# A closer spacing of the expert-row dots of half A beside half B's first mixer and queries: 226 of them ahead of half B's picks, where there were 138

## The reference, cut to what matters

```python
top_s, top_i = lax.top_k(s, PEER_TOPK)
...
best_s, best_pos = lax.top_k(cand_s.reshape(T, PEER_HEADS, PEER_TOPK * PEER_TOPK), PEER_TOPK)
...
u = expert_u[idx]
v = expert_v[idx]
act = jax.nn.gelu(jnp.einsum('td,thkd->thk', xb, u).astype(jnp.float32), approximate=False)
return jnp.einsum('thk,thkd->td', (gate * act).astype(xb.dtype), v)
```

## Time and profile before

| | |
|---|---|
| median of 3 runs | 4008.97 us (4008.68, 4008.97, 4033.02) |
| the profiled execution's own time | 4005.37 us |
| its span, first to last instruction | 4003.6 us |
| mean granted TensorE clock | 0.817 |
| busy over the span | PE 2671.4, DVE 2233.9, POOL 1309.2, ACT 531.7 us |
| half A's steps, from the first output tile of half B's mixer | from 504 to 1402 us |

### The profile page before, as it was taken

The page is one execution under the profiler, slowest core; times in us unless marked ns, Lnnn a source line. Parts: engine busy times, 40 slices in busy tenths (PEclk is TensorE's granted clock), DMA queues, the critical chain, the costliest instruction groups (busy, mean ns, idle before and its releaser), DMA issues. The chain is left out here.

```text
span 4003.6 us, 44680 instructions
## 1 busy us (share of the span) xinstructions
PE 2671.4 (67%) x17677; PEld 1952.8 (49%) x17677; DVE 2233.9 (56%) x4113; ACT 531.7 (13%) x1037; POOL 1309.2 (33%) x1088
## 2 busy tenths in 40 slices
PE   2768356779910067799947550398999778587774
PEld 2567245564400055688835440276888556332231
DVE  5342698768689967788759689624222553200001
ACT  0130002100000012222211000032222210000001
POOL 0000045457777755566635467200000000100000
PEclk6788678889955577899967775698999789699997
DMA  8222188679999988799876889532333222799996
GB/s 316 74 74 84 37 280 303 232 270 368 364 386 388 374 312 286 241 345 348 306 245 196 314 315 372 208 93 71 102 101 84 83 95 76 317 425 428 428 428 286
DMA packets 445584, 1006.32 MB, mean 251 GB/s; under 512 B 30397, under 2 KB 291911, under 8 KB 431047
## 3 DMA queue, kind: packets, MB, share of 16 engines
q0 software_dynamic: 151200, 549.54, 37.2%
q1 hardware_dynamic: 263524, 419.24, 29.0%
q10 hardware_dynamic: 30659, 34.80, 2.5%
HBM read 972.01 MB, written 31.47 MB: 251 GB/s over the span
## 5 line engine op out<-in xcount | busy, mean ns | idle before, releaser
L1234 POOL DMA_INDIRECT ring<-in_peer_u_dram,index x512 | 667.0, 1303 | 796.3 <-POOLq L190 361.7
L1234 POOL DMA_INDIRECT ring<-in_peer_v_dram,index x512 | 605.3, 1182 | 338.6 <-DVE h_rows_b L1300 138.7
L334 PE MATMUL bank<-hT,weights 128*128 128x256 f32 x2240 | 512.6, 394 | 162.7 <-DMA weights<-in_w_in_dram 73.0
L334 PEld LDWEIGHTS bank<-hT,weights 128*128 128x128 f32 x2240 | 443.7, 199 | 231.8 <-issue 94.2
L1482 PE MATMUL bank<-hT,weights 128*128 128x256 f32 x1792 | 420.6, 390 | 47.2 <-DVEq L149 22.6
L1482 PEld LDWEIGHTS bank<-hT,weights 128*128 128x128 f32 x1792 | 337.1, 193 | 97.2 <-issue 48.9
L1300 DVE SCALAR_TENSOR_TENSOR h_rows_b<-ring,coef,h_rows_b 128x1024 f32<-128x1024 f32 x254 | 325.7, 1282 | 31.5 <-SPq L132 6.4
L1294 DVE SCALAR_TENSOR_TENSOR ring<-ring,h_rows_a 128x1024 f32<-128x1024 f32 x256 | 308.7, 1224 | 56.0 <-DMA ring<-in_peer_u_dram,index 51.6
L1294 DVE SCALAR_TENSOR_TENSOR ring<-ring,h_rows_b 128x1024 f32<-128x1024 f32 x256 | 298.2, 1221 | 9.7 <-SPq L132 9.7
L2661 PE MATMUL bank<-xp_ring,weights 128*64 128x512 f32 x1024 | 254.1, 654 | 69.5 <-DMA xp_ring<-in_w_exp_gate_dram 48.9
L2445 POOL MEMSET weights<- 128x1024 f32 x1 | 1.0, 957 | 868.6 <-POOLq L160 868.6
(11 more groups left out here) (500 smaller groups left out, 4009.6 us busy)
## 6 DMA issues: line engine op xcount, KB each, us to landing
xp_ring<-in_w_exp_gate_dram SPq DMA_DIRECT2D x16, 4096.0 KB, 35.6
xp_ring<-in_w_exp_up_dram SPq DMA_DIRECT2D x16, 4096.0 KB, 33.3
xp_ring<-in_w_exp_down_dram SPq DMA_DIRECT2D x16, 4096.0 KB, 33.8
weights<-in_w_in_dram SPq DMA_DIRECT2D x112, 512.0 KB, 4.2
weights<-in_w_in_dram SPq DMA_DIRECT2D x54, 1024.0 KB, 11.3
ada_rows<-in_w_ada_dram SPq DMA_DIRECT2D x16, 1536.0 KB, 10.6
weights<-in_w_out_dram SPq DMA_DIRECT2D x16, 1024.0 KB, 5.2
weights<-in_peer_w_query_dram SPq DMA_DIRECT2D x16, 1024.0 KB, 5.8
```

What stands on the lines that cost most here:

```text
L334: ins = pe.matmul(m.ps[b][:, 0:TH], m.weights[:, s, k, c * P:(c + 1) * P], rhs(k), start=(k == 0), stop=(k == k_tiles - 1))
L1234: pool.indirect_dma_start(out=self.ring[:, n % RING, :], out_offset=None, in_=self.tables[table], in_offset=bass.IndirectOffsetOnAxis(ap=s ...
```

## The change

The spacing of the steps that lie ahead of the picks becomes a number of its own, `FRONT_PACE` = 1.1 us, where it was `PACE` = 1.8. `FRONT` goes from 138 to 226. After `reach_front` the spacing is 1.8 again. The number of steps, gathers, sums and diagonals is the same.

```diff
-PACE = 1.8
-PE_PACE = 0.75
+PACE, FRONT_PACE, PE_PACE = 1.8, 1.1, 0.75
...
-    FRONT = 138
+    FRONT = 226
...
-        self.n, self.activated, self.time, self.n_pe, self.pe_now = 0, 0, 0.0, 0, False
+        self.n, self.activated, self.time, self.n_pe, self.pe_now, self.pace = 0, 0, 0.0, 0, False, FRONT_PACE
...
         while self.n < self.FRONT:
             self.step(dve)
-        self.pe_now = True
+        self.pe_now, self.pace = True, PACE
...
-        while self.time >= PACE:
+        while self.time >= self.pace:
             if not self.can(2 * self.HALF_STEPS):
                 self.time = 0.0
                 break
-            self.time -= PE_PACE if self.on_pe(*self.plan[self.n][0:2]) else PACE
+            self.time -= PE_PACE if self.on_pe(*self.plan[self.n][0:2]) else self.pace
             self.step(dve)
```

## The result

| | median of the runs | lowest to highest | profiled execution | its span | mean clock |
|---|---|---|---|---|---|
| before | 4010.21 us | 4008.68 to 4033.02 (4) | 4005.37 us | 4003.6 us | 0.817 |
| changed | 3971.57 us | 3965.79 to 3978.95 (4) | 3965.79 us | 3964.1 us | 0.822 |

The changed kernel is faster: its time is 0.9892 of the time before, with a 95% interval from 0.9852 to 0.9931, which is 38.6 us. The forecast was 3967, and its range 3942 to 4000 holds the result. The time is nearly the one forecast, but it is not made up in the forecast's way, as the stages show.

The account below looks back on a forecast made before the run. It saw DVE, then mixed limits, then PE bound successive stages, then 108 us of DVE's dots with PE idle. 107.7 saved - 55.6 for DVE - 10 for transfers = 42 us less: 4009.0 becomes 3967, range 3942 to 4000.

Parts of the forecast that it names:

- The burst: End of the handover: 88 dots leave `finish`, so tile 1's coefficients wait for PE's last sum; 107.7 us saved.
- Rival 4: Tile 0's sums begin with a ring less full, PE ends later, less is saved; no chance of its own.
- DVE's sum: First projection to keys: 88 dots added to DVE's stages cost 55.6 us, bounds 26.6 and 100.3.
- The transfers: Second projection, norm with queries, and keys: gathers exceed the DMA engines' room; 10 us taken from 0 to 26.
- each overrun can be put off into the next stage, which has room: Stages ahead of the picks: the ring's 12 rows, 16.0 us of transfers, let excess transfers move into the next stage.
- The overrun of 12: Second projection: 89 us of transfers in a stage that DVE would leave after 77, 12 too many.
- My reason for the low end: Ahead of 883 us no dot waited for its row at two per tile, so the ring is full; 10 us taken.
- the keys: Keys stage: two dots beside DVE's 11.2 us wait for the keys cost only +1 us.
- Rival 1: Stages ahead of the picks: transfers bound them; 10 us saved, 3999, spread 3986 to 4010; chance 0.20.
- Rival 2: Projections: PE's clock falls to 1.2 GHz, 75 us slower, 4084; chance 0.07, plus 0.05 for a few slow tiles.
- the prediction's premise for it: Second projection: DVE sets the pace at 3.97 us per tile; PE idles 0.5 us in each, waiting for a bank.
- Rival 3: Stages ahead of the picks: dots fill more idle time; 75 us saved at most, 3934, likelier 3950; chance 0.08.

Follow-up runs that it names:

- experiment 3: Changed kernel with the old spacing 1.8 in the first projection, 210 dots ahead of the picks; 4014.1 us against the changed kernel's 4019.5.
- Experiments 2 and 4: Changed kernel with one load moved each: half B's `w_out` weights from the recurrence's start, 5.3 us faster; keys issued ahead of the queries' projection, 22.9 us faster.
- before again: Kernel before, unedited, profiled once more on the second chip; 4060.8 us.
- before, loads moved: Kernel before (138 dots, spacing 1.8) with keys loaded ahead of the queries' projection and half B's `w_out` from the recurrence's start; 17.3 us faster, ratio 0.9957.
- spacing 1.4: Changed kernel with 1.4 in place of 1.1 us between dots, 177 dots ahead of the picks, loads not moved; 22 us below before.
- change again: Changed kernel, unedited, profiled once more on the second chip; 39.4 us faster than before there.
- change, second time: Changed kernel, unedited, once more on the third chip; 39.7 us faster than before there.
- experiment 5: Changed kernel with keys early and `w_out` later, 33.5 us faster; its last kernel adds spacing 1.8 in the first projection (210 dots), 9.5 us longer than that.

## Why the prediction came right, and which term did not

**The burst.** Right: 107.7 forecast, 109.4 - 0.6 = 108.8 measured from PE's end, less 0.9 since picks with tile 0's sums took 231.0 in place of 230.1. The picks did not suffer, and tile 1's sums are at 178.9. Rival 4 falls.

**DVE's sum.** Right where DVE sets the pace: first projection +17.2 for +17.1, `hgrn` +16.3 for +15, projection by `w_out` with the norm +11.1 for +8, and DVE's busy time in the second projection as worked out. The first projection's dots are paid for one by one (experiment 3).

**The transfers: mis-sized.** The step that failed is "each overrun can be put off into the next stage, which has room", with 10 us taken from a range of 0 to 26. Measured are 32.4, more than the upper bound: 23.9 - 12.5 = 11.4 in the second projection, 0.1 in the first, 1.3 in `hgrn`, 3.1 in the projection by `w_out` with the norm, and 15.2 + 4.3 - 3 = 16.5 in the queries and the keys. The overrun of 12 that I had worked out for the second projection is nearly the 11.4 measured, and the 9 and 5 behind it stand against 19.6, of which 7.2 are the keys' longer wait. So the sums of bytes were about right and the deferral was wrong. Some 6 of the 32.4 show as no wait for a transfer and may as well belong to DVE's terms. A gather that is late is waited for at once, for DVE has no other work to put ahead of it; the ring's 12 rows cover a late start of the stage, and not a pitch of 1.70 against 1.25 kept up for 28 gathers, 47 us (an estimate: 28 x 0.45 = 12.6 us; DVE waited 9.6). My reason for the low end, that no dot waited for its row before, was read at two dots per tile, where there was 0.7 us of slack in each tile. It tells nothing of three. The second miss in this term is the keys: I put 11.2 us of wait down as a cover for two dots, while it is a wait for a transfer that took longer in the fuller traffic, and it became 18.6.

**Rival 1**, transfers that bound the stages, had 0.20 and holds in its mechanism: DVE waited for rows ahead of the picks (19.3 us in all, just under the 20 that were to be its sign; 9.6 us, 21 times, in the second projection alone), and PE 7.8 us for query weights (5.0 before). It had put the price at 42 us in all, of which 26 for the overruns and 16 for the weights; the first came true and little of the second. By the stretch alone its time was the nearer one: the profiled execution less 19.9 us is 3985.5, at the edge of the rival's 3986 to 4010. Experiments 2 and 4 show the cause, and 25 us of front come back when two loads are moved.

**Rival 2**, the clock, falls, and so does the prediction's premise for it, that PE would idle 0.5 us in each tile and wait for DVE. The window's mean clock fell from 0.96 to 0.83, under the 0.9 that I had named, but not while PE worked. PE's timeline in the second projection, and the two parts of its window:

```profile
595.59 50.97 PE L334 MATMUL bank<-hT,weights 128*128 128x256 f32 x224 [51.71 <-ACTq L142]
650.93 8.86 PE L334 MATMUL bank<-hT,weights 128*128 128x256 f32 x32 [4.38 <-DMA weights<-in_w_in_dram]
```
```profile
595.50:645.00 49.50, 49.41 (x218) 43.20 (x219) 46.84 (x93) 0.00 (x0) 36.50 (x27) 0.95 0.95 344
645.00:683.80 38.80, 10.41 (x40) 8.21 (x38) 30.59 (x52) 0.00 (x0) 31.79 (x24) 0.67 1.04 394
```

PE makes 14 of its 16 tiles in a row into the free banks (when the 14th ends, at 646.6, DVE has copied nine), waits once, for weights, and has nothing to do for the last 24 us, while DVE catches up. In the first part the clock is 0.95 (0.96 in the whole stage before); the 0.67 of the second part holds the idle end. The Trainium skill's rule on short idle times between groups of matmuls ("TensorE: Matmul & The Clock Gate", section "A second HAM failure mode: psum-queue depth-cycling") is not put to the test by this trace, for no such idle times stand between these 14 tiles, nor between the first 12 of the queries. **Rival 3** falls: no stage cost less than its sum.

**What I had not counted.** The stretch shows 19.9 us (30.8 on the second chip), the medians 38.6, 39.4 and 39.7. The rest lies outside. Some 6.5 of it came in every profile with 226 dots. Behind tile 1's sums, SP issues the four loads of the next `w_in`, and this takes

```
before 15.10   before again 14.21   before, loads moved 16.08   spacing 1.4 15.65   first projection old 16.52
changed 9.10   change again 9.51    change, second time 9.39    w_out later 9.56
```

The four profiles left lie at the same two levels: 9.2 to 10.0 in the three with 226 dots, 15.0 in the last kernel of experiment 5, with 210.

The time from the end of the sums to the first output of that projection is 53.2 to 55.2 us in the first row's kernels (and 54.7 in the last kernel of experiment 5), and 47.4 to 48.3 in all seven with 226 dots. Two profiles, in PE's timeline ahead of that projection, before and changed:

```profile
1418.78 5.17 PE L389 MATMUL bank<-hT,ones 128*128 128x256 f32 x16 [12.18 <-ACT hT L377]
```
```profile
1383.94 6.13 PE L389 MATMUL bank<-hT,ones 128*128 128x256 f32 x16 [6.17 <-ACT hT L377]
```

The first norm there stands behind a meeting of the engines at which SP comes last. Why SP is held some 6 us longer with 138, 177 or 210 dots was not tried, but all thirteen profiles agree in one thing. With 226 dots the ring is full when tile 1's sums end: POOL issued their last gather 16.4 us earlier, it issues only 3 more beside SP's four loads, and then it stands still until DVE frees a slot. With fewer dots the last gather was issued 10.0 to 12.3 us before the end, and 6 to 8 go out beside SP's loads. POOL's first stop behind the sums, before and changed:

```profile
1408.54 1.68 POOL L1234 DMA_INDIRECT ring<-in_peer_u_dram,index  x1 [0.80 <-DVE ring L1294]
```
```profile
1379.69 1.68 POOL L1233 DMA_INDIRECT ring<-in_peer_u_dram,index  x1 [4.53 <-DVE ring L1293]
```

That SP's issuing is slowed by the gathers beside it is therefore likely and not shown: no run changed the one without the other. The head, 8.9 us shorter in the first pair, is mostly chance: in the thirteen profiles it lies between 489.5 and 504.4, and one kernel alone shows 494.6 and 499.2. That leaves 12 us of the 38.6 in the first pair (the head's share among them) and 2 of the 39.4 in the second (30.8 + 6.5 = 37.3) that no lasting part of the traces accounts for.

So the forecast's time was met with a term 22 us too small and a gain of about that size beside it that was not forecast, 12 us of which no run explains. The mechanism, burst against front, was right, and the sum's agreement to 5 us is partly luck.

## What to carry to other kernels

Work moved into a stage's idle time earns only as long as both its engine and its transfers have room there; price each step by the stage's limit, and stop where the price per item reaches what an item saves (here 1.16 saved for 0.77 paid up to a spacing of 1.4, then 1.28 for 1.19). Where the sum of transfers exceeds a full stage, charge the excess to that stage (here 12 worked out, 11.4 measured), and do not count a wait for a transfer as idle time to be filled: here it grew from 11.4 to 18.6 us with the traffic. After such a change look for the loads that stand beside it: issuing one early and one late (no instruction more) took off 33.5 us, of which 24.9 lie in the stretch where the loads are. Most of it is the early one (22.9 and 17.4); for the late one a shorter front is shown and a shorter time is not.

## What was not expected of the hardware

- With 4 MB of weights in flight, an indirect gather of 128 rows kept POOL for 1.40 us and the gathers came 1.70 us apart; without them POOL had it done in 0.94 to 1.34.
- The weights themselves suffered more: `w_out`'s loads landed after 37.9 us, in a window in which `w_in`'s took 17.1.
- A small load can take nearly as long as a large one (`w_in`'s 1 MB loads took 17.1 us): of the keys' four loads of 256 KB the slowest landed after 15.6 us in the change (median 12.9) and after 8.3 before (6.1). Issued 82 us earlier, at 844, the slowest took 15.1 (median 6.4), and nothing waited for it.
- Behind tile 1's sums, issuing four loads took SP 9.1 to 10.0 us with 3 gathers beside it (seven profiles) and 14.2 to 16.5 with 6 to 8 (six profiles). The cause is open.
- PE does not follow DVE's pace tile by tile: with DVE taking 3.76 to 5.04 us per tile, PE still made 14 tiles in 50.97 us at a granted clock of 0.95 and idled at the end. The mean clock of a window says little where it holds such an end.
